# One table load per step pair on the DMA queue's engine, and the last normalised tile stored ahead of two weight chunks

## The reference, cut to what matters

```
logits = (h @ router_w + router_b)
top_v, top_i = top_k(logits, 4);  top_w = softmax(top_v)
per expert e, for its tokens:
    z = h[tok] @ w1[e] + b1[e]            # 1024 -> 2048
    z_glu = min(z_glu, 7);  z_lin = clip(z_lin, -7, 7)
    act = z_glu * sigmoid(1.702 * z_glu) * (z_lin + 1)
    y = act @ w2[e] + b2[e]               # 1024 -> 1024
out = rmsnorm(h_lat + g2 * sum(top_w * y))
```

## Time and profile before

| | us |
|---|---|
| median of 3 runs | 1643.22 (1639.86 to 1646.82) |
| the profiled execution | 1641.11 |
| span of its trace | 1638.9 |
| granted TensorE clock over the span, share of full speed | 0.951 |
| expert loop in the trace | about 536 to 1592 |
| SP's table reads (two steps), line 480 alone | 168 loads |

### The profile page before, as it was taken

One profiled execution on the slowest core, in us unless ns is written; L12 is line 12 of the kernel. 1 busy time (PEld: TensorE's weight loads), 2 busy tenths in 40 slices (PEclk: granted clock), 3 DMA queues, 4 the chain that ended last, 5 costly groups with the idle time before them and its releaser, 6 DMA issues.

```text
span 1638.9 us, 40839 instructions
## 1 busy us (share of the span) xinstructions
PE 1485.2 (91%) x14640; PEld 739.0 (45%) x14640; DVE 734.8 (45%) x2468; ACT 251.8 (15%) x434; POOL 211.9 (13%) x263
## 2 busy tenths in 40 slices
PE   5999999999894988999899799999788979898897
PEld 3658888888552332333244234333233323343233
DVE  4403877776747442434244244434233424343344
ACT  4403554554322000000000000000000000000001
POOL 1000000000250111212121111212111211111120
PEclk9999999999996998999799799999899989999898
DMA  8685111112767898948989989999899989999788
GB/s 358 194 269 146 52 52 51 51 51 55 277 266 265 338 419 320 417 199 337 414 325 400 414 336 400 417 414 412 320 418 416 417 324 410 417 413 417 298 323 310
DMA packets 130870, 497.14 MB, mean 303 GB/s; under 512 B 15372, under 2 KB 48492, under 8 KB 94908
## 3 DMA queue, kind: packets, MB, share of 16 engines
q1 hardware_dynamic: 122588, 479.99, 74.3%
q0 software_dynamic: 8256, 16.81, 2.8%
HBM read 484.92 MB, written 17.58 MB: 307 GB/s over the span
## 4 chain that ended last, share of the span: by engine, by line
PE 62%; DMA 22%; SPq 9%; DVE 4%; issue 3%; ACT 1%; POOL 0%; DVEq 0%; POOLq 0%; ACTq 0%
PE ps L1788 22%; PE ps L1826 12%; DMA arena<-in_moe_w 10%; DMA big_b<-in_moe_w 10%; PE ps L1485 6%; PE ps L1487 5%; PE ps L1486 5%; SPq L435 3%; SPq L429 3%; PE ps L1664 2%; PE ps L1596 1%; PE ps L1508 1%; DMA ring_t<-in_mod_c 1%; PE ps L1610 1%; PE ps L1605 1%
## 5 line engine op out<-in xcount | busy, mean ns | idle before, releaser
L1788 PE MATMUL ps<-arena,rows 128*32 128x512 f32 x2736 | 330.2, 617 | 41.8 <-DMA arena<-in_moe_w 33.4
L1788 PE MATMUL ps<-big_b,rows 128*32 128x512 f32 x2688 | 318.7, 609 | 29.6 <-DMA big_b<-in_moe_w 29.2
L1788 PEld LDWEIGHTS ps<-arena,rows 128*32 128x32 f32 x2736 | 86.4, 112 | 239.3 <-issue 151.2
L862 ACT ACTIVATE rows<-ps 128x256 f32<-128x256 f32 x84 | 32.3, 385 | 1050.1 <-issue 566.3
L1788 PEld LDWEIGHTS ps<-big_b,rows 128*32 128x32 f32 x2688 | 85.0, 111 | 220.2 <-issue 149.0
L1826 PE MATMUL ps<-big_b,rows 128*32 128x256 f32 x2688 | 166.4, 398 | 15.3 <-DMA big_b<-in_moe_w 15.3
L1826 PE MATMUL ps<-arena,rows 128*32 128x256 f32 x2688 | 167.0, 400 | 13.8 <-DMA arena<-in_moe_w 13.8
L1403 DVE SCALAR_TENSOR_TENSOR y_sb<-ps,w_s,g_q 128x256 f32<-128x256 f32 x42 | 20.3, 484 | 293.2 <-PE ps L1826 293.2
L1403 DVE SCALAR_TENSOR_TENSOR rows<-ps,w_s,g_q 128x256 f32<-128x256 f32 x42 | 20.3, 484 | 279.0 <-PE ps L1826 279.0
L1826 PEld LDWEIGHTS ps<-big_b,rows 128*32 128x32 f32 x2688 | 84.2, 114 | 77.6 <-DMA big_b<-in_moe_w 21.7
L1826 PEld LDWEIGHTS ps<-arena,rows 128*32 128x32 f32 x2688 | 84.8, 114 | 75.7 <-DMA arena<-in_moe_w 20.3
(11 more groups left out here) (361 smaller groups left out, 1769.6 us busy)
## 6 DMA issues: line engine op xcount, KB each, us to landing
big_b<-in_moe_w SPq DMA_DIRECT2D x192, 1024.0 KB, 15.4
arena<-in_moe_w SPq DMA_DIRECT2D x192, 1024.0 KB, 16.7
ring_t<-in_hg_w_in SPq DMA_DIRECT2D x32, 512.0 KB, 3.9
ogT<-in_mod_w SPq DMA_DIRECT2D x16, 1024.0 KB, 5.1
arena<-yrows SPq DMA_DIRECT2D x8, 1024.0 KB, 12.0
x_sb<-in_x SPq DMA_DIRECT2D x2, 2048.0 KB, 7.9
arena<-in_hg_w_in SPq DMA_DIRECT2D x4, 1024.0 KB, 21.0
arena<-in_mod_c SPq DMA_DIRECT2D x4, 1024.0 KB, 22.3
```

Of the source, the lines that this page charges most:

```text
L1788: last = mm(bank[q * G:(q + 1) * G, :], XT[par][:, pos * G:(pos + 1) * G], w[:, :, q * NW:(q + 1) * NW], start=(pos == 0), stop=False)
```

## The change

Three edits. First, the two tables become one, `tab_words`, in which each block's expert and mark stand side by side behind two unused words; SP reads six words (three blocks) with one load at the head of an iteration, for both steps, and the runtime checks of the words' range are left out. Second, `f_scaled` and `f_shifted` become one `f_tile`, so tile 3 is shifted before the router's work on DVE, and `store(LT - 1)` moves ahead of the wait for the logits and of two w1 chunks. Third, `transpose_x(0, 16)` moves ahead of four products on DVE.

```
-        tab_l, tab_new = (nc.alloc_sbuf_tensor_at(n, [1, NBT], I32, offset=place["res"] + 4 * NW + 4 * i * NBT)
-                          for i, n in enumerate(("tab_l", "tab_new")))
+        tab_words = nc.alloc_sbuf_tensor_at("tab_words", [1, 2 * NBT + 2], I32, offset=place["res"] + 4 * NW)
+        tab_ld = tab_words[:, 2:2 * NBT + 2].rearrange("p (b w) -> p b w", w=2)
...
             for k in range(2):
                 load_w2(0, 0, k)
+            store(LT - 1)
             sp.wait_ge(S["lg_ps"], LT)
             for pos in range(3, 5):
                 load_w1(1, 1, pos)
-            store(LT - 1)
             load_w2(0, 0, 2)
...
             with sp.Fori(0, n_pairs) as i:
+                _, words = nc.values_load_multi_w_load_instructions(
+                    tab_words[0:1, bass.ds(i * 4 + 4, 6)], engines=[mybir.EngineType.SP], min_val=0, max_val=E - 1,
+                    skip_runtime_bounds_check_because="experts are clamped to E - 1 and marks are 0 or 1 where written")
                 for par in range(2):
...
-                    e_next, new_next = entry(1)
-                    e_over, new_over = entry(2)
+                    e_next, new_next = words[2 * par:2 * par + 2]
+                    e_over, new_over = words[2 * par + 2:2 * par + 4]
...
-            f_scaled(LT - 1)
+            f_tile(LT - 1)
...
             V.tensor_copy(msk16[:, :, :], msk).then_inc(S["msk_ok"], 1)
-            f_shifted(LT - 1)
...
-            me.mark(V.tensor_scalar(tab_l[:, :], bef[0:1, :], float(E - 1), None, ALU.min))
+            me.mark(V.tensor_scalar(tab_ld[:, :, 0], bef[0:1, :], float(E - 1), None, ALU.min))
...
-            me.link(V.tensor_copy(tab_new[:, :], tab_nf))
+            me.link(V.tensor_copy(tab_ld[:, :, 1], tab_nf))
...
             index(1, False)
+            transpose_x(0, 16)
             for k in range(TOPK):
                 me.mark(V.tensor_tensor(ohd[:, :, k, :], oh[:, :, k, :],
                                         kf4[:, :, k:k + 1].broadcast_to([P, LT, E]), ALU.mult))
-            transpose_x(0, 16)
```

More of the change, by code:

```diff
@@ L1165, in attn_out, with f_tile @@
                 V.tensor_tensor(x_sb[:, i, c0], x_sb[:, i, c0], y, ALU.add).then_inc(S["h_ok"], 1)
-            def f_scaled(i):
+            def f_tile(i):
                 dve.wait_ge(S["h_ok"], added(i + LT))
@@ L1175, in f_scaled @@
                                                ALU.mult, ALU.mult))
-            def f_shifted(i):
                 V.tensor_tensor(f_two[:, i % 2, :], f_two[:, i % 2, :], sh2_row, ALU.add).then_inc(S["f_ok"], 1)
-            def f_tile(i):
-                f_scaled(i)
-                f_shifted(i)
             def hT_copy(i):
```

## The result

The changed kernel takes 1623.87 us (median of 4 runs, 1622.66 to 1628.61), the kernel before, run beside it, 1642.65 us (4 runs, 1639.86 to 1646.82). The ratio is 0.9901, with a 95% interval of 0.9876 to 0.9925, which is 12 to 20 us. The profiled execution took 1622.66 us with a span of 1620.8, against 1641.11 and 1638.9: 18.1 us of span. The forecast was 15.5 us and 1627.7 us.

The account below looks back on a forecast made before the run. The prediction took PE and the weight stream, restarted late by SP's table reads, as the bound. Loop 10.6 plus store 4.9 gave 15.5 us, so 1643.2 - 15.5 = 1627.7 us; range 1619 to 1638.

Parts of the forecast that it names:

- What bounds the kernel: Expert loop: PE and weight stream bound it; where PE waits, a 1 us earlier stream start brings PE 1 us forward.
- a pace of its own: Rival, loop: the stream's own pace at a start sets PE's waits, so only the store counts; 1638.3 us, chance 0.08.
- The odd starts: Loop starts at 650.80 and 744.41: odd steps read nothing, so loads go 1.6 us earlier each, 3.2 us together.
- B and C: PE's positions at 752.15 and 888.75, behind the two counted odd starts; 1.6 us forecast for each start.
- The even starts: Starts at 881.76, 985.67, 1184.77, 1351.23: gain 2.5 - L, L the six-word read's time, taken as 0.9; four times 1.6 us.
- D to G: PE's positions at 1047.14, 1191.84, 1306.77 and 1515.82, behind the four counted even starts; 6.4 us forecast together.
- The first start: Load at 546.63: SP some 4 us earlier, but earlier loads keep engines busy except 546.6 to 547.6; gain 1.0 us.
- A: PE's position at step 11 (680.27), behind the first counted start and PE's first waits after it; 1.0 us forecast.
- Starts that don't count: Odd starts at 848.39 and 952.46, with no PE wait before the queue dries again, and 1552.41: 0 us.
- The loop's sum: Gains of first, two odd and four even starts in the expert loop: 10.6 us, bounds 7.3 to 14.5.
- The store: Ahead of the loop: earlier tile-3 store lets the gather wait for the index, PE starting 4.9 us earlier (3.5 at least).
- PE's waits fall by 10 us: Sign of the prediction: PE's waits for weights, as a total, fall by about 10 us.

Follow-up runs that it names:

- `wait_even`: Changed kernel plus five checked single-word reads, values unused, at the head of each even step: 1638.89 us, 0.9992 of the kernel before.
- `wait_odd`: Changed kernel plus five checked single-word reads, values unused, at the head of each odd step: 1632.28 us, 0.9949 of the kernel before.
- `reads_only`: Kernel before with only the one table and six-word load; store, shift and transpose as before: 1629.08 us, 0.9930 of the kernel before.
- `unchecked`: Changed kernel with four single-word reads in each step from the one table, without range checks: 1627.33 us, 0.9927 of the kernel before.
- `each_step`: Changed kernel with one four-word read in each step instead of six words per pair: 1622.77 us, 0.9901 of the kernel before.
- empty delays: Changed kernel with four unused six-word reads added at even or odd steps, left out of the program, so unchanged: 0.9915 and 0.9908 of the kernel before.
- `before_again`: Kernel before, unchanged, run again for a second trace: ratio 0.9996.
- `store_only`: Changed kernel with the two tables and four checked reads a step put back; early store, shift and transpose stay: 1635.62 us, 0.9970 of the kernel before.
- `four_two`: Changed kernel with its six-word read split into four words at the even step and two at the odd: 1622.65 us, 0.9896 of the kernel before.
- `late_transpose`: Changed kernel with the first transpose put back behind the four products on DVE: 1626.70 us in a single run.
- the repetitions: Second executions of both kernels, unchanged: the kernel before at ratio 0.9996, the changed kernel at 1626.25 us, 0.9919 of the kernel before.

## Why the prediction was right, point by point

**What bounds the kernel.** Right, by `wait_even` and `wait_odd`: a start that comes later costs PE about as much behind it, and a start that is left alone costs little or nothing. Had the stream a pace of its own at a start, the late starts would have cost nothing.

**The odd starts.** 1.6 us each was forecast; the issue moved from 2.71 to 1.09 us behind the bias matmuls, 1.63. Behind B and C `reads_only` gains 1.57 and 1.54 us, the changed kernel 0.3 to 1.3 and 1.7 to 1.9 in four executions.

**The even starts.** The rule gain = 2.5 - L was right, with 1.6 us for a load of L = 0.9. The load takes 0.72 us, and the start moved by 1.94 (3.39 to 1.45): 1.8 by the rule, and 0.15 for the range check's work behind the last read, which I had only in the upper bound. At D to G `reads_only` gains 1.7, 0.7, 1.5 and 2.2 us, 6.1 for my 6.4, and 0.8 more behind G. By the six words' 0.72 us the rule of 200 ns for each register, an L of 1.2 us, doesn't hold here; it is stated for loads from HBM (the Trainium skill, Runtime: NRT & Kernel Launch, Instruction fetch mechanics), and this table lies in SBUF.

**The first start: a term too small.** I gave 1.0 us (0.7 to 1.3), the length of the window with no DMA work. Measured at A are 2.4 to 2.6 us (the changed kernel, four executions) and 2.5 us (`reads_only`). My step "DMA stands still only in 546.6 to 547.6" counted the hole and not its slopes. Windows of the kernel before on both sides of it:

```profile
541.00:546.60 5.60, 5.60 (x92) 2.73 (x88) 0.94 (x6) 0.00 (x0) 0.00 (x0) 1.00 0.91 366
...
547.60:551.60 4.00, 4.00 (x44) 1.27 (x40) 3.08 (x14) 0.38 (x1) 2.06 (x2) 1.00 0.94 338
```

The same of the changed kernel, where SP's first load goes out at 537.35:

```profile
537.35:541.20 3.85, 3.85 (x75) 2.36 (x76) 0.00 (x0) 0.00 (x0) 0.00 (x0) 1.00 1.02 409
...
542.30:546.00 3.70, 3.70 (x44) 1.19 (x40) 2.77 (x12) 0.39 (x1) 2.06 (x2) 1.00 1.02 423
546.00:552.00 6.00, 6.00 (x96) 2.83 (x92) 0.96 (x5) 0.00 (x0) 0.00 (x0) 1.00 1.01 415
```

Before, 541.0 to 551.6 moved 366 x 5.6 + 338 x 4.0 = 3.40 MB; at the 415 GB/s of the last window it would be 4.40. The missing 1.0 MB is 2.4 us, and that is the gain. The other kernels agree that the gain ends there. The first load goes out 9.87 us behind the entry's bias matmuls before, and PE's gain at A is 0.6 to 0.7 us where it goes out 1.3 us sooner (the two waits), 2.1 where 1.9 (`unchecked`), 2.3 where 3.6 (`each_step`), and 2.4 to 2.6 where 3.8 to 4.8 us sooner.

**Starts that don't count.** Nearly right. The odd starts at 848.39 and 952.46 were left out. With them 2.1 us later, `wait_odd` loses up to 0.9 us at D and 1.4 to 1.8 at E, so the second may count in part; a column of one execution drifts by as much, so the size stays open.

**The loop's sum.** Forecast 10.6 (7.3 to 14.5). From the measured shifts, 2.4 + 2 x 1.63 + 4 x 1.94 = 13.4 us; from the positions 13.0, 11.9 and 12.5, and 13.1 and 11.3 in the empty delays. Against the mean of the three executions with the old reads (`before`, `before_again`, `store_only`), the mean of these five is 12.1 us ahead: 2.4 at the first start (1.0 forecast), 3.1 at the two odd ones (3.2) and 6.6 at the four even ones, to the end of the loop (6.4). So the loop is 1.5 us above the forecast, and 1.4 of them are the first start.

**The store.** 4.9 us was forecast (3.5 to 4.9). PE's first expert matmul moved from 526.72 to 521.02, 5.7 us, but 0.9 of them stood already before the router: its first work on DVE (`MAX8`, 506.49 and 506.20) came 0.3 us earlier, although the shift now ahead of it costs the forecast 0.6. From there to PE's matmul it is 20.23 us before and 14.82 after, 5.4 us less, of which that 0.6 is taken back: 4.8. Each step held in this pair: the index became what the gather waits for, 0.02 us separates the gather's landing from the second index, and the products' move is worth 0.7 (0.8 by the prediction). One pair of executions says no more than that. From the scaling of tile 3 to PE's first expert matmul it is 22.0 to 22.8 us in the three executions with the late store and 17.8 to 18.3 in the ten with this prologue: 4.55 us between the means. To the loop's entry it is 32.2 and 28.0, only 4.3 us. The prediction passed the whole on; but the 48 matmuls at that place take longer in the changed kernel (8.12 us for 7.57), at a granted clock of 0.65 for 0.70. So this term came out 0.6 us too large. The margins of the tie are thin: in `four_two` the store landed last, 0.4 us behind the index, and the gather waited for it:

```profile
514.00 1.04 POOL L624 DMA_INDIRECT rows<-frows,tok_n  x1 [24.42 <-DMA frows<-ring_t]
```

The 0.9 us above are not the change's: in the profiled executions of the kernels above with this same prologue (all but the one before and `reads_only`, and `late_transpose`) the entry lies anywhere from 529.5 to 535.3.

**What would show it.** 42 reads, an odd start 1.27 us behind its step's first w1 matmul (1.15 forecast), dry windows shorter by 1.5 to 3.1 us (1.6 forecast), the gather on `row_n` (at 514.3 rather than 515.2) and an idle 3.26 us: seen. PE's waits were to fall by about 10 us and fell by 7.9 us (91.7 to 83.8); the repetitions have 89.1 and 83.6. There I took all of the loop's gain for waits, but 5.3 us of it is PE's busy time. That part is the clock. PE's busy time in the loop times the granted clock, summed over windows of 0.5 us, is 923 to 925 us in every execution above, so PE's work at full clock is the same in all. What differs is its idle time and what the lower clock costs (its busy time times what the clock lacks of 1.00): 93.0 and 48.2 us before, 90.2 and 52.1 in `before_again`, 85.2 and 43.4 in the changed kernel, 84.8 and 44.8 in its repetition, 87.9 and 54.1 in `wait_even`. The lower clock comes behind clusters of waits, as here in the kernel before, where 64 w2 matmuls take 5.34 us, and 3.66 where nothing was waited for:

```profile
700.63 1.06 PE L1788 MATMUL ps<-big_b,rows 128*32 128x512 f32 x8 [1.79 <-DMA big_b<-in_moe_w]
701.82 5.34 PE L1826 MATMUL ps<-arena,rows 128*32 128x256 f32 x64
...
883.55 3.66 PE L1826 MATMUL ps<-big_b,rows 128*32 128x256 f32 x64
```

The sum of the two parts is what repeats: 140 to 142 us with the old reads, 129 to 131 in the four executions of the changed kernel, 142 in `wait_even`. How it splits differs from one execution to the next. This fits the prediction's mechanism, in which the stream sets PE's time in such a stretch and PE loses it either idle or at the lower clock; the sign "PE's waits fall by 10 us" was the wrong thing to look for.

**What is left over.** Behind G the changed kernel gains another 2.6 us, its repetition 0.8 and `reads_only` 0.8. But the unchanged kernel's second execution gains 2.7 there and `store_only`, with the old reads, 1.5, so this is mostly a draw of the executions, and of the first one of the kernel before. The four spans of the changed kernel (1620.8, 1622.4, 1625.0 and 1627.2) are 14.6 us below the two of the kernel before (1638.9 and 1638.1) in the mean, so the profiled 18.1 us are some 3 us above what the change gives. The medians of the changed kernel's four measurements, the two empty delays among them, say 13.8 to 18.8 us. The forecast of 15.5 lies among them partly by luck: the loop gave 1.5 us more than its term and the store 0.6 less.

## What to carry to other kernels

Where a stream of transfers is issued by one in-order engine and runs dry, the time of its next start is that engine's instructions between the release and the issue, and it passes to the consumer nearly one for one, but only in stretches where the consumer waits at all; list the starts, and count the ones with a wait behind them. A small read of a table by the issuing engine belongs outside that path, and its range check costs time too (here 0.25 us on top of 0.37). The gap of a dried-up stream is better measured as missing bytes over the full rate than as the length of its idle window; here that was seen at one start. And where the stream sets the time, count the consumer's idle time and its time at the lower clock together.

## What the runs showed of the hardware

- On SP, a load of one word from SBUF takes 0.27 us and of six words 0.72 us. Four words take 0.30 us in the even steps of `each_step` (295 ns at the least), where they begin on a multiple of 16 bytes from the table's start, and 0.87 us in the odd ones, where they begin 8 bytes behind one. Two words from such a multiple took 0.47 us in the odd steps of `four_two`. So the time isn't a price for each word. What sets it wasn't tried beyond this.
- A read with its range check takes 0.62 us from one to the next, one without about 0.37.
- After a dry queue the first 1 MB load lands 4.8 to 5.1 us after its issue (six starts before, five after), while at the 400 to 420 GB/s of a stream that runs 1 MB takes 2.5 to 2.6 us.
- TensorE's granted clock fell to 0.50 seventeen times in the loop of the kernel before, each time behind waits for weights. In the loops above the lower clock costs 43 to 54 us, beside 83 to 93 us of idle time.
